# Weight slabs of half depth and double width, with a fourth place in the ring, in a two-layer decoder trunk

## The chip, the cores and the metric

The kernel runs on one core of a Trainium2 chip, in fp32 throughout. The time is the device time of one execution in microseconds (us). A core has a TensorE (PE) for matrix products, VectorE (DVE), ScalarE (ACT) and GpSimd (POOL) for the rest, and 16 DMA engines that move data between HBM and the on-chip memory SBUF. SyncE (SP) only issues transfers here. Products land in PSUM, eight banks of 512 fp32 columns by 128 partitions, written `PS[:, bank, column]`.

## The reference, cut to what matters

The trunk has 512 tokens of width 1024 and two layers. Each layer is a mixer and then a PEER channel mixer. The first mixer has gated channels and sparse attention, the second is a gated linear recurrence with 8 heads.

```python
def peer(x, w_q, sub_keys, u_tab, v_tab):
    def block(xb):
        qh = (xb @ w_q).reshape(P_TOK_BLOCK, P_HEADS, 2, P_QDIM // 2)
        s = jnp.einsum('thpd,hpnd->thpn', qh, sub_keys).astype(jnp.float32)
        s_top, i_top = lax.top_k(s, P_TOPK)
        ...
        experts = jnp.take_along_axis(cand_idx, pos, axis=-1)
        gate = jax.nn.softmax(best, axis=-1).astype(xb.dtype)
        u = u_tab[experts]
        v = v_tab[experts]
        act = jax.nn.gelu(jnp.einsum('td,thkd->thk', xb, u))
        return jnp.einsum('thk,thkd->td', gate * act, v)

def even_mixer(h, w_in, ...):
    u, v, q, kc, vc, ks, vs, kw, vw, gt = jnp.split(h @ w_in, EVEN_SPLITS, axis=-1)
    a = chunked_gmlp(jax.nn.gelu(u), jax.nn.gelu(v), a_ln_w, a_ws, a_bs)
    b = nsa(...)
    return jnp.concatenate([a, b], axis=-1) @ w_out
```

Each token thus reads 128 rows (8 heads by 16 experts) of u and v in each layer.

## The kernel before

**Slots.** The experts' work is cut into 1024 slots. A slot is one expert for each of 128 tokens: POOL gathers a row of u and v for every partition (8 KB each, 1 MB in all) into one of 8 buffers (`gath`, L646), DVE takes the dot product with x (L1282), ACT turns it into a weight and scales a diagonal matrix by it (L909, L910, L916), and PE adds the weighted v rows by two products with that diagonal (`row_product`, L1777; a few slots are added by DVE instead). A buffer comes free after that. A phase is 256 slots.

**Ticks.** All other work runs between the slots. On every engine the pieces of mixers and routings are generators that yield a tick; a piece runs ahead of the slot whose number is its tick. The 512 tokens are four blocks of 128; a mixer works on two blocks at a time ("q"), and so does a routing ("job"). The first mixer for q=0 and the routing of its first heads come before slot 0, q=1 of the first mixer has ticks 12 to 170 of phase 0, beside heads 2 to 7 of routing job 0. Routing job 1 follows late in phase 0. Phases 1 and 2 each hold one q of the second mixer and then one routing job (2 and 3), and phase 3 has slots alone.

**Slabs.** Weights come in slabs of 1 MB, loaded by SP in the fixed order of `order_` (L386), which is sorted by tick. Before slot 0 seven places in the gather buffers serve (`first_slabs`); from then on three places in `region_a`, used in turn. Before SP loads slab i it waits until the user of slab i-3 is done (`slab`), and PE waits for the landing (`slab_there`). In the first mixer the slabs of q=1 are: F 0 to 3 (keys, queries and compressed keys and values, products L1367), G (L1376), C 0 and 1 (L1390), V 0 and 1 (L1474), U 0 and 1 (L1489), O 0 to 3 (output, L1668). A routing head h needs slab R: 256 columns of `w_q` for all 8 chunks of 128 rows, and 128 KB of keys behind them (L453). F, V, U and R slabs are 256 columns wide, so each partition receives 8 pieces of 1 KB. C, O and the second mixer's H slabs are 8 KB in one piece per partition.

**Routing on PE.** Head h has four parts of four products (L1605) at ticks `route_tick(job, h)` to +3, then ACT copies the query, and at +5 four products with the keys (L1616), whose event `r_sc` frees the slab. In jobs 1 to 3 the heads are 7 ticks apart, in job 0 (from head 2) 14.

`positions_in_pairs` (L470) copies compressed keys and values within SBUF by 16 small transfers for q=1; SP issues them ahead of slab C 0.

Of the kernel before, what the change touches and what calls it, by code (L numbers as in the profile page):

```python
# [76 lines left out]
def build(nc, x, wcol_mix, w_ffn, w_fin, w_even, ln_w, ws_t, b_s, pos, ck1, ck2, cv1, cv2, w_out_e,  # L77
# [8 lines left out]
    with ExitStack() as ctx:  # L86
# [51 lines left out]
        slabs = [carve(RA, i * SLAB, SLAB) for i in range(3)]  # L138
# [100 lines left out]
        f_done, f_out, g_done, g_out = (event(n) for n in ("f_done", "f_out", "g_done", "g_out"))  # L239
# [28 lines left out]
        slab_in = [sem(f"slab_in{i}") for i in range(3)]  # L268
# [94 lines left out]
        def even_slabs(q):  # L363

            t = EVEN_AT[q]
            out_ = [(t + 12 + 8 * i, ("F", q, i), (f_done, 4 * q + i)) for i in range(4)]
            out_ += [(t + 44, ("G", q), (g_done, q))]
            out_ += [(t + 52 + 8 * kv, ("C", q, kv), ((c_half, q), (hid_done, q))[kv]) for kv in range(2)]
            out_ += [(t + 68 + 8 * i, ("V", q, i), ((v_half, q), (v_done, 2 * q + 1))[i]) for i in range(2)]
            out_ += [(t + 84 + 8 * i, ("U", q, i), ((u_half, q), (u_done, 2 * q + 1))[i]) for i in range(2)]  # L370
            return out_ + output_slabs(q, t + ATT + 48)

        def output_slabs(o, t):
            return [(t + 4 * j, ("O", o, j), (pw_used, 3 * o + j) if j < 3 else (pw_done, 4 * o + 3)) for j in range(4)]

        def routing_slabs(job):
            return [(route_tick(job, h), ("R", job, h), (r_sc, P_HEADS * job + h)) for h in range(P_HEADS)]

        def odd_slabs(q):

            out_ = [(head_tick(q, h) - 16 + half_ if h else head_tick(q, 0) - 8, ("H", q, h, half_),
                     (ig_done, C_HEADS * q + h)) for h in range(C_HEADS) for half_ in range(2)]
            return out_ + output_slabs(2 + q, head_tick(q, 7) + 3)

        first_order = even_slabs(0)
        order_ = even_slabs(1) + routing_slabs(0) + routing_slabs(1)  # L386
        for q_ in range(2):
            order_ += odd_slabs(q_) + routing_slabs(2 + q_)
        order_.sort(key=lambda e: e[0])
        first_at = {name: i for i, (_, name, _) in enumerate(first_order)}  # L390
        slab_at = {name: i for i, (_, name, _) in enumerate(order_)}
        slab_user = [user for _, _, user in order_]
        first_user = [user for _, _, user in first_order]

        def with_keys(i):
            return order_[i][1][0] == "R"

        def slab_level(i):
            return sum(16 + 16 * with_keys(j) for j in range(i % 3, i + 1, 3))

        def slab_of(*name):

            if name in first_at:
                return first_slabs[first_at[name] % 7]
            return slabs[slab_at[name] % 3]

        def slab_there(eng, *name):
# [4 lines left out]
            else:  # L412
                i = slab_at[name]
                eng.wait_ge(slab_in[i % 3], slab_level(i))
# [3 lines left out]
        def _(sp):  # L418
# [4 lines left out]
            def dram_of(name):  # L423

                kind, i = name[0], name[-1]
                if kind == "F":
                    lo = TM_ALL + (768, 0, 256, 512)[i]
                    return w_even[:, :, lo:lo + HALF]
# [4 lines left out]
                if kind == "V":  # L433
                    return w_even[:, :, 512 + i * HALF:512 + (i + 1) * HALF]
                if kind == "U":
                    return w_even[:, :, i * HALF:(i + 1) * HALF]
# [4 lines left out]
                return w_q[name[1] // 2][:, :, i * HALF:(i + 1) * HALF]  # L441

            def load(dst, name, there):
# [7 lines left out]
                if name[0] == "R":  # L451
                    _, job, h = name
# [3 lines left out]
            def first_slab(i):  # L456
# [4 lines left out]
                load(first_slabs[i % 7], first_order[i][1], first_in[i % 7])  # L461

            def slab(i):

                if i >= 3:
                    ev, n = slab_user[i - 3]
                    sp.wait_ge(ev.sem, ev.at(n))
                load(slabs[i % 3], order_[i][1], slab_in[i % 3])

            def positions_in_pairs(q):  # L470

                sp.wait_ge(f_out.sem, f_out.at(4 * q + 3))
# [32 lines left out]
            for i in range(3, len(order_)):  # L505
                if order_[i][1] == ("C", 1, 0):
                    positions_in_pairs(1)
                if order_[i][1] == ("H", 0, 0, 0):
# [146 lines left out]
        def _(act):  # L655
# [3 lines left out]
            def even_pieces(q):  # L659
# [25 lines left out]
                for i in range(4):  # L685
                    yield t0 + 20 + 8 * i
                    act.wait_ge(f_done.sem, f_done.at(4 * q + i))
                    src = v3(PS[:, 2 + i % 2, :], 2)
                    if i == 0:
                        last = a.activation(kT[:, :, q * HALF:(q + 1) * HALF], src, ACT.Copy)  # L690
                    elif i < 3:
                        last = a.activation(qT[:, 2 * i - 2:2 * i, :], src, ACT.Copy)
                    else:
                        if q == 0:
                            a.activation(kvl[:], src[:, :, HALF - CMP_STRIDE:HALF], ACT.Copy)
                        last = a.activation(kvc, src, ACT.Copy)
                    last.then_inc(f_out.sem, 1)
# [644 lines left out]
        def _(pe):  # L1342
            t = nc.tensor

            def even_pieces(q):
# [10 lines left out]
                for i in range(4):  # L1356
                    W = slab_of("F", q, i)[:, 0:KC * HALF].rearrange("p (c n) -> p c n", n=HALF)
                    for part in range(4):
                        yield t0 + 12 + 8 * i + 2 * part
                        if part == 0:  # L1360
                            slab_there(pe, "F", q, i)
                            pe.wait_ge(n_hT.sem, n_hT.at(2 * q + 1))
                            if i >= 2:
                                pe.wait_ge(f_out.sem, f_out.at(4 * q + i - 2))
                        o = part // 2
                        for c in range(4 * (part % 2), 4 * (part % 2) + 4):
                            k_ = t.matmul(PS[:, 2 + i % 2, o * HALF:(o + 1) * HALF], W[:, c, o * P:(o + 1) * P], hTe[:, c, :],  # L1367
                                          start=c == 0, stop=c == KC - 1)
                    k_.then_inc(f_done.sem, 1)
# [487 lines left out]
```

## Time and profile before

| | us |
|---|---|
| median of 3 runs | 3161.55 |
| lowest and highest | 3159.0, 3165.18 |
| the profiled execution | 3163.08 |
| its span from first to last instruction | 3161.1 |
| PE busy | 2742.0 (87%) |
| DVE, ACT, POOL busy | 2218.8, 1521.1, 1292.2 |
| gather queue q0 | 147456 packets, 1073.81 MB, 83.1% of 16 engines |
| SP's queue q1 | 69792 packets, 118.83 MB, 10.1% |

Rows of the section further down come from one profiled execution. "Idle before" in brackets is the time in which an engine waited, with what ended it. In the windows view the DMA share is the mean busy share of the 16 DMA engines. It goes a little over 1, since packets overlap, so 1.01 or 1.02 means full.

### The profile page before, as it was taken

The page shows a single profiled execution, that of the slowest core. Times are in us where ns is not written, and L with a number is a line of the kernel's source. Part 1 is how long each engine was busy: PE and PEld are TensorE (multiplying, and loading weights), DVE is VectorE, ACT ScalarE, POOL GpSimd, SP SyncE. Part 2 cuts the span into 40 slices and gives each one's busy share as a digit, 9 for nine tenths or more (in the row PEclk, how much of TensorE's full clock was granted, in tenths as well). Part 3 has the DMA queues.
Part 4 walks back from the last instruction along what each step waited for, and adds up shares of the span by engine and source line. Part 5 has one row for each costly group of instructions (what it writes and reads, how often), then busy time and mean ns, then how long its engine had stood idle before and what let it go on. Part 6 is the DMA issues. An engine that isn't in the chain of part 4 may idle for free.

```text
span 3161.1 us, 30483 instructions
## 1 busy us (share of the span) xinstructions
PE 2742.0 (87%) x8496; PEld 1484.4 (47%) x8496; DVE 2218.8 (70%) x5543; ACT 1521.1 (48%) x4080; POOL 1292.2 (41%) x1254
## 2 busy tenths in 40 slices
PE   8979789899897998889898898989999878878887
PEld 7545556344454555554465455545455422222222
DVE  1347457885766787888776788788776777676664
ACT  2334244785443556555443465565544444444443
POOL 0014234442443444445443445444544444434432
PEclk9889899999998999999999999999999999999999
DMA  8039899998999999999999999999999999999997
GB/s 290 4 116 421 316 401 390 395 345 328 403 418 422 409 378 388 382 375 398 403 421 419 421 418 363 377 402 378 396 419 417 398 427 427 427 419 421 427 427 330
DMA packets 217418, 1194.57 MB, mean 378 GB/s; under 512 B 21537, under 2 KB 77857, under 8 KB 79521
## 3 DMA queue, kind: packets, MB, share of 16 engines
q0 software_dynamic: 147456, 1073.81, 83.1%
q1 hardware_dynamic: 69792, 118.83, 10.1%
q8 instruction: 68, 1.11, 0.1%
q14 instruction: 102, 0.83, 0.1%
HBM read 1189.38 MB, written 2.10 MB: 377 GB/s over the span
## 4 chain that ended last, share of the span: by engine, by line
PE 44%; DMA 24%; DVE 14%; ACT 9%; issue 5%; POOL 3%; SPq 0%; DVEq 0%; POOLq 0%; ACTq 0%
PE ps L1777 24%; DMA region_g<-in_uv_dram,experts 18%; DVE region_g L1282 6%; DMA region_a<-in_keys_dram 6%; PE ps L1605 5%; PE ps L1637 3%; PE ps L1668 3%; POOL region_g L646 2%; ACT x_res L916 1%; PE ps L1367 1%; ACT L909 1%; PE ps L1567 1%; PE ps L1634 1%; PE ps L1685 1%; DVE region_a L1084 1%
## 5 line engine op out<-in xcount | busy, mean ns | idle before, releaser
L1777 PE MATMUL ps<-region_g,x_res 128*128 128x512 f32 x3712 | 1815.3, 621 | 270.8 <-ACT x_res L916 240.1
L646 POOL DMA_INDIRECT region_g<-in_uv_dram,experts x1024 | 1166.9, 1140 | 1651.8 <-PE ps L1777 1341.1
L1282 DVE CUSTOM_DVE_ANT_0 region_g<-region_g,region_h 128x1024 f32<-128x1024 f32 x1024 | 1256.3, 1230 | 504.3 <-DMA region_g<-in_uv_dram,experts 490.8
L1777 PEld LDWEIGHTS ps<-region_g,x_res 128*128 128x128 f32 x3712 | 689.9, 196 | 1104.1 <-issue 565.2
L909 ACT ACTIVATE region_a<-region_a 128x1 f32<-128x1 f32 x1024 | 206.5, 202 | 1249.3 <-DVE region_a L1282 1244.3
L916 ACT ACTIVATE x_res<-ident,region_a 128x128 f32<-128x128 f32 x928 | 373.3, 402 | 30.4
L910 ACT ACTIVATE region_a<-region_a,gate 128x1 f32<-128x1 f32 x1024 | 302.7, 296 | 33.4
L1605 PE MATMUL ps<-region_a 128*128 128x256 f32 x1024 | 251.7, 393 | 46.6 <-DMA region_a<-in_keys_dram 45.4
L1605 PEld LDWEIGHTS ps<-region_a 128*128 128x128 f32 x1024 | 200.2, 197 | 121.0 <-DMA region_a<-in_keys_dram 51.7
L909 ACT ACT_TABLE_LOAD x128 | 164.2, 1283 | 12.7 <-DVE region_a L1282 10.5
L1634 PE MATMUL ps<-region_a 128*128 128x256 f32 x512 | 134.0, 392 | 1.0 <-DVE region_a L1118 1.0
L1634 PEld LDWEIGHTS ps<-region_a 128*128 128x128 f32 x512 | 102.5, 201 | 66.9 <-issue 58.2
L1291 DVE SCALAR_TENSOR_TENSOR x_res<-region_g,region_a,x_res 128x1024 f32<-128x1024 f32 x96 | 123.1, 1282 | 10.4 <-ACT region_a L910 10.4
L1637 PE MATMUL ps<-region_a 128*128 128x256 f32 x512 | 129.1, 379 | 0.0
L1637 PEld LDWEIGHTS ps<-region_a 128*128 128x128 f32 x512 | 96.7, 190 | 58.0 <-issue 50.7
L1668 PE MATMUL ps<-region_a 128*128 128x512 f32 x192 | 88.8, 592 | 0.0
L1282 DVE DVE_READ_ACCUMULATOR2_ANT region_a<- 128x1 f32 x1024 | 84.7, 83 | 0.0
L901 ACT ACT_TABLE_LOAD x63 | 80.8, 1283 | 1.1
L1165 DVE SCALAR_TENSOR_TENSOR region_a<-ps,ost,region_a 128x128 f32<-128x128 f32 x32 | 9.7, 346 | 89.0 <-POOL ost L533 57.1
L1685 PEld LDWEIGHTS ps<-region_a 128*128 128x128 f32 x512 | 66.4, 191 | 10.5 <-POOL region_a L612 5.1
L1094 DVE COPY_PREDICATED region_a<-level_mask,ps 128x256 f32<-128x256 int32 x128 | 56.7, 443 | 19.9 <-PE ps L1685 11.7
L1685 PE MATMUL ps<-region_a 128*128 128x128 f32 x512 | 67.8, 276 | 2.7 <-POOL region_a L612 2.5
(233 smaller groups left out, 2305.5 us busy)
## 6 DMA issues: line engine op xcount, KB each, us to landing
region_a<-in_w_q_dram SPq DMA_DIRECT2D x32, 1024.0 KB
region_a<-in_w_odd_dram SPq DMA_DIRECT2D x32, 1024.0 KB
region_g<-in_uv_dram,experts POOLq DMA_INDIRECT x1024
region_g<-in_w_even_dram SPq DMA_DIRECT2D x8, 1024.0 KB, 8.2
region_a<-in_w_even_dram SPq DMA_DIRECT2D x8, 1024.0 KB
region_a<-in_w_out_o_dram SPq DMA_DIRECT2D x8, 1024.0 KB
region_a<-in_keys_dram SPq DMA_DIRECT2D x32, 128.0 KB
region_g<-in_w_out_e_dram SPq DMA_DIRECT2D x4, 1024.0 KB, 7.8
```

The lines of the kernel that those rows point to most:

```text
L646: g.indirect_dma_start(out=gath[:, s % NBUF, :], out_offset=None, in_=uv[s // (2 * PHASE)], in_offset=bass.IndirectOffsetOnAxis(ap=experts ...
L909: link(a.activation(gact[:, c:c + 1], dots[:, c:c + 1], ACT.Gelu_apprx_tanh))
L910: i = a.activation(wts[:, c:c + 1], gact[:, c:c + 1], ACT.Copy, scale=gate[:, n % 2, k:k + 1])
L916: a.activation(diag[:, pe_n(s) % NBUF, :], ident, ACT.Copy, scale=wts[:, c:c + 1]).then_inc(diag_ready.sem, 1)
L1282: v.tensor_tensor_reduce(out=u_, in0=u_, in1=XNr[n // P_HEADS % 3], scale=1.0, scalar=0.0, op0=ALU.mult, op1=ALU.add, accum_out=dots[:, c: ...
L1291: v.scalar_tensor_tensor(xb, gath[:, s % NBUF, D_MODEL:ROW], wts[:, c:c + 1], xb, ALU.mult, ALU.add).then_inc(vd_done.sem, 1)
L1605: i = t.matmul(PS[:, 4, p * HALF:(p + 1) * HALF], W[:, c, p * P:(p + 1) * P], hTh[:, c, :], start=c == 0, stop=c == KC - 1)
L1634: i = t.matmul(PS[:, 2, o * HALF:(o + 1) * HALF], W[:, c % 4, o * P:(o + 1) * P], hTh[:, c, :], start=c == 0, stop=c == KC - 1)
L1637: i = t.matmul(PS[:, 3, o * HALF:(o + 1) * HALF], hTh[:, c, o * P:(o + 1) * P], W[:, c % 4, HALF:2 * HALF], start=c == 0, stop=c == KC - 1)
L1668: i = t.matmul(PS[:, out_bank(o, bank), :], headT[:, c, r * P:(r + 1) * P], W[:, c % 2, half_ * 512:(half_ + 1) * 512], start=c == 0, stop ...
L1685: i = t.matmul(PS[:, 4 + pair % 2, (lev % 2) * HALF + r * P:(lev % 2) * HALF + (r + 1) * P], k_, q_, start=True, stop=True)
L1777: i = t.matmul(PS[:, j, :], diag[:, pe_n(s) % NBUF, :], gath[:, s % NBUF, D_MODEL + j * 512:D_MODEL + (j + 1) * 512], start=first, stop=last)
```

## The change

R, V and U slabs and two of the F slabs now hold 4 chunks of 128 rows instead of 8, and 512 columns instead of 256, so a partition receives 4 pieces of 2 KB. The bytes of a slab stay the same. Two routing heads share a pair of such slabs (`("R", job, pair, half)`): both heads need both, the keys of the even head lie behind the first and those of the odd head behind the second. The first half is freed by the odd head's `r_q`, the second by its `r_sc`. In jobs 1 to 3 odd heads run one tick earlier. F 2 and F 3 hold all queries and add up into banks 6, 7, 2 and 3; F 1 now holds the compressed keys and values, so `positions_in_pairs` waits for `f_out` 1 instead of 3 and is issued ahead of F 3. V and U products are 512 columns wide, half as many. A fourth place lies over `headT`, used in the first mixer of q=1 alone from `pw_done` 3 on (all output pieces of q=0 done). The order of phase 0 and the place of each slab are written by hand; later ones use three places in turn.

```diff
-        slabs = [carve(RA, i * SLAB, SLAB) for i in range(3)]
+        slabs = [carve(RA, i * SLAB, SLAB) for i in range(3)] + [carve(RA, 3 * SLAB + KC * HALF, KC * HALF)]
...
-            return NORM_TICK[job] + 9 + 7 * h
+            return NORM_TICK[job] + 9 + 7 * h - h % 2
...
+        def routing_slabs(job, pair):
+            n = P_HEADS * job + 2 * pair + 1
+            return [(("R", job, pair, 0), (r_q, n)), (("R", job, pair, 1), (r_sc, n))]
...
+        order_ = [(*R0[0][0], 0), (*R0[0][1], 1), (*F0, 2), (*F1, 3), (*R0[1][0], 0), (*R0[1][1], 1), (*F2, 2),
+                  (*R0[2][0], 0), (*R0[2][1], 1), (*F3, 3), (*G_, 2), (*C0, 3), (*R0[3][0], 0), (*R0[3][1], 1), (*C1, 2),
+                  (*V0, 3), (*V1, 2), (*U0, 3), (*U1, 2), (*O0, 0), (*O1, 1), (*O2, 2), (*O3, 0)]
...
+        order_ += [(*e, (i + 1) % 3) for i, e in enumerate(later)]
...
-                sp.wait_ge(f_out.sem, f_out.at(4 * q + 3))
+                sp.wait_ge(f_out.sem, f_out.at(4 * q + 1))
...
-                if order_[i][1] == ("C", 1, 0):
+                if order_[i][0] == ("F", 1, 3):
                     positions_in_pairs(1)
...
+                for half_ in range(2):
+                    W = slab_of("F", q, 2 + half_)[:, 0:KC * HALF].rearrange("p (c n) -> p c n", n=2 * HALF)
+                    for part in range(4):
+                        yield t0 + 28 + 8 * half_ + 2 * part
+                        if part == 0:
+                            slab_there(pe, "F", q, 2 + half_)
+                        if part >= 2:
+                            pe.wait_ge(f_out.sem, f_out.at(4 * q + part - 2))
+                        for c in range(4 * half_, 4 * half_ + 4):
+                            k_ = t.matmul(PS[:, (6, 7, 2, 3)[part], 0:HALF], W[:, c % 4, part * P:(part + 1) * P], hTe[:, c, :],
+                                          start=c == 0, stop=c == KC - 1)
...
+                        pe.wait_ge(f_out.sem, f_out.at(4 * q + 2))
...
                         yield route_tick(job, h) + part
+                        if part < 2:
+                            slab_there(pe, "R", job, h // 2, part)
```

On SP, from the last slab of q=0 on, the order before was this (`in_w_even` with 8x256 is F, with 8x280 G; `in_w_q` is R):

```order
L450 DMA region_a<-in_w_even_dram 128x8x256 [waits r_sc]
L450 DMA region_a<-in_w_q_dram 128x8x256 [waits r_sc]
L453 DMA region_a<-in_keys_dram 128x256
L450 DMA region_a<-in_w_even_dram 128x8x256 [waits r_sc]
L450 DMA region_a<-in_w_even_dram 128x8x256 [waits f_done]
L450 DMA region_a<-in_w_q_dram 128x8x256 [waits r_sc]
L453 DMA region_a<-in_keys_dram 128x256
L450 DMA region_a<-in_w_even_dram 128x8x256 [waits f_done]
L450 DMA region_a<-in_w_even_dram 128x8x280 [waits f_done]
```

These are F 0, R of head 3, F 1, F 2, R of head 4, F 3 and G. Now, from the same place on (F 0 is loaded before):

```order
L459 DMA region_a<-in_w_even_dram 128x8x256 [waits pw_done]
L459 DMA region_a<-in_w_q_dram 128x4x512 [waits r_q]
L463 DMA region_a<-in_keys_dram 128x256
L459 DMA region_a<-in_w_q_dram 128x4x512 [waits r_sc]
L463 DMA region_a<-in_keys_dram 128x256
L459 DMA region_a<-in_w_even_dram 128x4x512 [waits f_done]
L459 DMA region_a<-in_w_q_dram 128x4x512 [waits r_q]
L463 DMA region_a<-in_keys_dram 128x256
L459 DMA region_a<-in_w_q_dram 128x4x512 [waits r_sc]
L463 DMA region_a<-in_keys_dram 128x256
L488 DMA region_a<-region_h 64x256 [waits f_out]
```

These are F 1, the pair of heads 2 and 3, F 2, the pair of heads 4 and 5, and the first of the 16 small transfers, which now stand ahead of F 3.

On PE, head 4 of job 0 began like this, with one wait for its slab (`slab_in1`) ahead of its first part:

```order
L1367 MATMUL ps<-region_a 128x256 x4
L1605 MATMUL ps<-region_a 128x256 [waits r_qo,r_hT,slab_in1]
L1605 MATMUL ps<-region_a 128x256 x3
L1777 MATMUL ps<-region_g,x_res 128x512 [waits diag_ready]
L1777 MATMUL ps<-region_g,x_res 128x512
L1605 MATMUL ps<-region_a 128x256 x4
```

Now:

```order
L1389 MATMUL ps<-region_a 128x256 x4
L1632 MATMUL ps<-region_a 128x256 [waits r_qo,r_hT,slab_in0]
L1632 MATMUL ps<-region_a 128x256 x3
L1804 MATMUL ps<-region_g,x_res 128x512 [waits diag_ready]
L1804 MATMUL ps<-region_g,x_res 128x512
L1632 MATMUL ps<-region_a 128x256 [waits slab_in1]
```

The head's first part waits for the first half of its pair, and the second part, one row product later, for the second half.

## Rows read from the trace of the kernel before

**Rows 1.** Page, DMA queues: packets, MB, share of 16 engines' span

```profile
q0 software_dynamic: 147456, 1073.81, 83.1%
q1 hardware_dynamic: 69792, 118.83, 10.1%
```

**Rows 2.** Windows: busy of each engine, granted clock, DMA share, GB/s

```profile
core 0: us, PE busy (x) PEld busy (x) DVE busy (x) ACT busy (x) POOL busy (x), PEclk, DMA share, GB/s
...
300.00:400.00 100.00, 76.12 (x258) 50.16 (x257) 52.46 (x135) 27.87 (x82) 26.11 (x25) 0.88 0.89 332
400.00:500.00 100.00, 89.68 (x356) 57.39 (x356) 60.09 (x150) 41.80 (x117) 33.34 (x32) 0.95 0.98 383
...
620.00:780.00 160.00, 149.02 (x450) 69.34 (x449) 118.87 (x275) 116.30 (x274) 68.98 (x73) 0.97 0.88 331
...
1540.00:1740.00 200.00, 182.63 (x583) 107.21 (x583) 139.67 (x337) 86.29 (x246) 87.76 (x74) 0.97 1.02 419
...
2500.00:3100.00 600.00, 477.51 (x958) 171.97 (x956) 423.37 (x1071) 262.54 (x784) 252.33 (x247) 0.97 1.01 425
```

**Rows 3.** Windows of 20 us within phase 0, same columns

```profile
300.00:320.00 20.00, 10.40 (x37) 6.55 (x35) 14.74 (x43) 6.50 (x21) 6.18 (x6) 0.89 1.02 418
320.00:340.00 20.00, 14.48 (x47) 10.22 (x48) 7.57 (x20) 2.58 (x6) 1.92 (x3) 0.77 0.64 224
340.00:360.00 20.00, 20.00 (x73) 13.01 (x72) 7.36 (x11) 9.32 (x27) 9.07 (x8) 1.00 0.92 343
...
380.00:400.00 20.00, 20.00 (x71) 13.79 (x71) 9.73 (x26) 3.86 (x10) 4.62 (x5) 0.90 0.83 269
...
480.00:500.00 20.00, 20.00 (x77) 13.77 (x76) 17.45 (x48) 10.80 (x27) 7.37 (x7) 1.00 0.87 310
```

**Rows 4.** Waits from 234 to 500 us: total, times, longest

```profile
POOL region_g L646 <- PE ps L1777: 164.0, 60, 19.5
...
PE ps L1605 <- DMA region_a<-in_keys_dram: 32.6, 3, 15.1
```

**Rows 5.** Timeline of PE in phase 0: start, length, line, idle before

```profile
308.51 1.89 PE L1367 MATMUL ps<-region_a 128*128 128x256 f32 x8
325.52 3.78 PE L1605 MATMUL ps<-region_a 128*128 128x256 f32 x8 [15.13 <-DMA region_a<-in_keys_dram]
...
330.91 1.89 PE L1605 MATMUL ps<-region_a 128*128 128x256 f32 x8
...
349.02 1.89 PE L1367 MATMUL ps<-region_a 128*128 128x256 f32 x8
...
378.74 3.78 PE L1605 MATMUL ps<-region_a 128*128 128x256 f32 x8 [8.76 <-DMA region_a<-in_keys_dram]
...
391.88 1.89 PE L1605 MATMUL ps<-region_a 128*128 128x256 f32 x8
...
422.45 1.89 PE L1605 MATMUL ps<-region_a 128*128 128x256 f32 x8
```

**Rows 6.** Timeline of PE, last two heads of routing job 2

```profile
1702.91 1.99 PE L1605 MATMUL ps<-region_a 128*128 128x256 f32 x8 [2.14 <-DMA region_a<-in_keys_dram]
...
1726.42 3.78 PE L1605 MATMUL ps<-region_a 128*128 128x256 f32 x8 [5.14 <-DMA region_a<-in_keys_dram]
```

**Rows 7.** Windows: routing slabs beside gathers, and gathers alone

```profile
1678.00:1697.00 19.00, 17.65 (x64) 11.02 (x63) 12.20 (x26) 8.95 (x23) 8.07 (x7) 1.00 1.02 417
2600.00:2800.00 200.00, 161.61 (x324) 57.34 (x322) 139.81 (x360) 87.75 (x263) 80.61 (x80) 0.97 1.01 427
```

**Rows 8.** Timeline of SP: slab issues in phase 0 and in routing job 2

```profile
250.15 28.95 SPq L450 DMA_DIRECT2D region_a<-in_w_even_dram  x2
...
1621.51 0.55 SPq L450 DMA_DIRECT2D region_a<-in_w_q_dram  x1
...
1639.61 0.55 SPq L450 DMA_DIRECT2D region_a<-in_w_q_dram  x1
```

**Rows 9.** Page, DMA issues: an 8 KB load, us from issue to landing

```profile
lbraw<-in_lbs_dram SPq DMA_DIRECT2D x1, 8.0 KB, 4.4
```

More of the change, by code:

```diff
@@ L363, in even_slabs @@
         def even_slabs(q):
[L365 to L377, printed above, removed]
+            out_ = [(("F", q, i), ((f_done, 4 * q), (f_done, 4 * q + 1), (f_half, q), (f_done, 4 * q + 3))[i]) for i in range(4)]
+            out_ += [(("G", q), (g_done, q))]
@@ L387, in build @@
-        for q_ in range(2):
[L388 to L399, printed above, removed]
+        F0, F1, F2, F3, G_, C0, C1, V0, V1, U0, U1, O0, O1, O2, O3 = even_slabs(1)
@@ new lines, in build @@
+        R0 = [routing_slabs(0, pair) for pair in range(4)]
+        order_ = [(*R0[0][0], 0), (*R0[0][1], 1), (*F0, 2), (*F1, 3), (*R0[1][0], 0), (*R0[1][1], 1), (*F2, 2),
+                  (*R0[2][0], 0), (*R0[2][1], 1), (*F3, 3), (*G_, 2), (*C0, 3), (*R0[3][0], 0), (*R0[3][1], 1), (*C1, 2),
+                  (*V0, 3), (*V1, 2), (*U0, 3), (*U1, 2), (*O0, 0), (*O1, 1), (*O2, 2), (*O3, 0)]
+        later = [e for pair in range(4) for e in routing_slabs(1, pair)]
+        for q_ in range(2):
+            later += odd_slabs(q_) + output_slabs(2 + q_)
+            later += [e for pair in range(4) for e in routing_slabs(2 + q_, pair)]
@@ new lines, in build @@
+        order_ += [(*e, (i + 1) % 3) for i, e in enumerate(later)]
+        order_ = [(name, slot, user) for name, user, slot in order_]
+        first_at = {name: i for i, (name, _) in enumerate(first_order)}
+        slab_at = {name: i for i, (name, _, _) in enumerate(order_)}
+        first_user = [user for _, user in first_order]
+        slab_before, slab_level, users, levels = [], [], [None, None, None, (pw_done, 3)], [0] * 4
+        for name_, slot_, user_ in order_:
+            slab_before.append(users[slot_])
+            users[slot_] = user_
+            levels[slot_] += 16 + 16 * (name_[0] == "R")
+            slab_level.append(levels[slot_])
@@ L440, in dram_of @@
                     return w_odd[name[2]][:, i * 2048:(i + 1) * 2048]
-                return w_q[name[1] // 2][:, :, i * HALF:(i + 1) * HALF]
+                _, job, pair, half_ = name
+                return w_q[job // 2][:, 4 * half_:4 * half_ + 4, pair * 512:(pair + 1) * 512]
             def load(dst, name, there):
@@ L451, in load @@
                 if name[0] == "R":
-                    _, job, h = name
+                    _, job, pair, half_ = name
+                    h = 2 * pair + half_
                     sp.dma_start(dst[:, KC * HALF:SLAB].rearrange("p (a b) -> p a b", a=2),
@@ L696, in even_pieces @@
                         last = a.activation(kvc, src, ACT.Copy)
+                    else:
+                        bank = (6, 2)[i - 2]
+                        last = a.activation(qT[:, 2 * i - 4:2 * i - 2, :], PS[:, bank:bank + 2, 0:HALF], ACT.Copy)
                     last.then_inc(f_out.sem, 1)
```

83 lines of the change are left out of this document (44 added, 39 removed).

## The prediction, written before the result was known

> **What bounds the kernel now.** I first read the DMA queues and the DMA share by stretch, then who stops whom where that share falls. Two queues share the 16 DMA engines: the gathers take 83.1% of the engines' time and SP's loads 10.1% [rows 1]. In the last phase, with gathers alone, the share is full and 425 to 427 GB/s flow [rows 2, 7]. During routing job 2 (1540 to 1740 us) it is full too, at 419 GB/s [rows 2]. So there DMA sets the time, and only fewer or cheaper bytes help. In phase 0 it isn't full: 0.89 from 300 to 400 us and 0.98 to 500 [rows 2]. Full is 1.02 here, and the four low windows of 20 us hold 20 x (0.38 + 0.10 + 0.19 + 0.15) = 16.4 us of idle DMA [rows 3]. From 620 to 780 us, at 0.88, PE is 93% busy with attention [rows 2], which this change doesn't touch.
>
> What leaves DMA idle in phase 0 is PE. From 234 to 500 us PE waits almost only three times, 32.6 us in all, for a routing slab whose keys come last, and POOL stands up to 19.5 us with no buffer free [rows 4]. Two of these waits are 15.13 and 8.76 us, and the four products after each take 3.78 us instead of 1.89 [rows 5]: the granted clock was at its lower level (1.2 GHz of 2.4) after the idle time, at 0.77 of full over 320 to 340 us [rows 3]. With 1.9 us for each, the waits cost PE 32.6 + 5.7 = 38.3 us.
>
> **Why the slabs come late.** In job 2 the last two heads both start on a landing, at 1702.91 and 1726.42 us [rows 6]: one slab of 1152 packets of 1 KB (keys included) per 23.5 us. At 417 GB/s [rows 7] 9.8 MB flow in that time, 1.18 MB of them slab, so the gathers move 8.6 MB, or 1055 packets of 8 KB. The engines thus alternate, about 1.09 slab packets for one gather packet. A gather packet takes 8192 B / (427/16 GB/s) = 307 ns. The 16 engines have 376 us in 23.5 us, so a 1 KB packet takes (376 - 1055 x 0.307) / 1152 = 45 ns.
>
> **Part 1, packets of 2 KB.** No row has one alone. It costs between 77 ns (bytes at the gathers' rate) and 90 ns (twice 45). I take 82, on the line through 45 and 307. A slab then needs 512 x 82 / 16 = 2.62 us of all engines instead of 2.88, or 0.26 us less (0 to 0.4). Beside gathers it lands in (512/1.09 x 0.307 + 512 x 0.082) / 16 = 11.6 us, plus 2.6 for the keys (an eighth of the old 20.9), so 14.2 instead of 23.5. The Trainium skill (Perfetto Trace Analysis, DMA Optimizations) says that transfers under 2 KB have a large overhead each and that batching them raises throughput a lot. By the line above the overhead of a packet is some 7 ns, and 0.26 us a slab is all the throughput there is; more of it would only add to the gain.
>
> **Part 2, jobs 1 to 3.** DMA is full, so 24 slabs give 24 x 0.26 = 6.3 us (0 to 9). A new wait comes with the pairs: the second half of the next pair is requested when the odd head's projection ends (`r_q`) and is needed 6 ticks later by the second part of the next head. A tick is 18.1/7 = 2.59 us (issues at 1621.51 and 1639.61 us [rows 8]), so there are 15.5 us. The load needs 4.4 us of latency (small load, [rows 9]) + 14.2 = 18.6. PE waits some 3 us, and up to 1.9 more where the clock falls. The loop from one `r_q` to the next is then 18.6 + 8 ticks (20.7) + 1.9 = 41.2 us at most, while DMA needs 14 gathers x 2.46 + 2 slabs x 2.98 = 40.4 for the same slots. The two are level and buffered by 8 gathers, so I book 0 for it (0 to 2 us for each of 9 waits). Behind the waiting PE stand row products, and behind those POOL's free buffers; SP's H slabs are asked for 4 ticks later and used 24 ticks on.
>
> **Part 3, phase 0.** F 1 and the pair of heads 2 and 3 are requested before or about the first gather, and the second half (14.2 + 4.4 us) is there by the time of head 2's second part. Then step by step, on the clock of before. F 2 is issued at 278.6 us as now (end of the double row at 250.15, [rows 8]), lands at 279 + 3 + 11.6 = 294, the first half of heads 4 and 5 at 308, the second at 322.5, and with the end of its latency PE has it at 325. PE reaches it after the F part at 308.51, one head part and one row product [rows 5], at 313.7: a wait of 11.5 us. At 325 it then starts the second part, which before ran at 330.91 [rows 5], so it is 5.5 us ahead. Next in the queue stand 16 small transfers, 1024 packets of at most 1 KB. Beside gathers they would hold F 3 back by 20.9 us, alone by 3. PE has just stood still for 11 us, which 8 buffers hardly outlast, so the gather queue is nearly dry: I take 3. F 3 lands by 341; PE needs it 349.02 - 330.91 = 18.1 us after 325 [rows 5], at 343: a wait of 0 to 14, I take 2. G is still 1 KB wide, issued two ticks earlier than the use of F 3, and just makes it: 0 to 4, I take 2. Head 5 shares head 4's pair, so the wait at 378.74 is gone, and so is the one at head 7. For heads 6 and 7 both halves are asked for within 5 us, the first at head 5's `r_q` (393.8, the end of the part at 391.88), and both are in after 4.4 + 2 x 14.2 = 32.8 us; PE is at the place of 422.45 after 28.7 [rows 5]: 4 us. Sum of waits: 11.5 + 2 + 2 + 4 = 19.5, and 3.8 for the clock at two of them, 23.3 in place of 38.3. PE gains 15 us. DMA: 16.4 idle + 11 slabs x 0.26 = 19.3 at most, less some 5 that stay idle after the 11.5 us wait and the later ones, 14. Neither limit lets more through than the smaller, and they won't mesh fully: I take 12 (bounds 0 and 19).
>
> **Part 4, the rest.** Before slot 0 nothing waits on a slab; the F, V and U products keep their columns (256 wide, eight rows in 1.73 us; 512 wide, twice that), and G's new wait for ACT's copy is covered by eight F products. Fewer weight loads run beside products. 0, bounds +-2. The fourth place waits for `pw_done` 3, which comes before head 0's keys; ACT writes `headT` again only after U 0. After 500 us the order of slabs is the old one.
>
> **Sum.** 12 + 6 = 18 us from the profiled execution's 3163.1, so 3145; the median lies 1.5 lower, so 3143.5, which I round to 3143.
>
> **The rivals.**
> (a) New waits eat phase 0. If the small transfers do meet live gathers, F 3 comes 14 us late, G behind it 4 or more, and PE's sum is 23.3 + 14 = 37 against 38.3. Only the 6 us of part 2 stay, or fewer: 3155 to 3162. For it: the second half lands when gathers restart. Against: POOL's 19.5 us without a buffer [rows 4].
> (b) DMA fills nearly everywhere: the full 19 in phase 0, 9 in the jobs, and a few from the drained spell after job 3: 3130 to 3135.
> (c) Slower: the share goes by bytes, not by packets, or the rows are split into 1 KB again. A slab then still needs 23.5 us, and the pairs turn this into a loss: the loop is 27.9 + 20.7 + 1.9 = 50.5 us against 40.4, over three waits in three jobs 91 us, of which 8 buffered slots a job (20 us) hide up to 60: about +30, so 3190. It decides from a landing time of about 13.5 us on, where the loop passes DMA's 40.4; my 14.2 is close to that, so even the expected time has a small loss in it. Against it: 1152 to 1055 packets is one to one in number and 1 to 7.3 in bytes, which a share by bytes would hit only by chance. The Trainium skill (DMA: Bandwidth & Descriptors, Queues, rings and completion order) says that an engine changes rings only after a whole packet of typically 9 to 17 descriptors; where such packets are cut by bytes, this rival follows, at its 3190. The profile's one to one count speaks for turns by the single row, or equal numbers of rows.
>
> **How the numbers follow.** Forecast 0.58 (3138 to 3155), (a) 0.22, (b) 0.10, (c) and other losses 0.10. Low 3128 takes in (b), high 3163 takes in (a), which leaves out about 0.17. A measurement of this kernel tells some 0.2%, 6 us, from no change. Faster by more: forecast, (b) and a quarter of (a), 0.73. Within: 0.16. Slower: 0.11.
>
> **What would show it.** Right: 2 KB packets at 80 to 85 ns; in jobs 1 to 3 short PE waits (3 to 5 us) at the second part of heads 2, 4 and 6, with the DMA share still at 1.02; in phase 0 one wait of about 11 us at head 4's second part, none at heads 5 and 7, and 500 us of before reached near 488. Wrong: long waits at F 3 or G (a), landings still 23 us apart (c), or a share under 1 inside the jobs, which would mean that the pair loop and not DMA sets the pace there.

## The result and the profile after

The change made the kernel slower, where a gain of 0.6% was forecast.

| | median, us | lowest to highest | runs |
|---|---|---|---|
| before | 3161.55 | 3157.35 to 3166.11 | 7 |
| after | 3184.69 | 3175.39 to 3196.53 | 7 |

The ratio is 1.0066, with a 95% interval of 1.0046 to 1.0086, so the loss is small but clear of no change. The profiled execution of after took 3188.32 us, its span is 3186.4. The forecast was 3143 with a range of 3128 to 3163, so the time lies outside of the range and on the other side of no change.

First the queues, from the page of after (packets, MB, share of 16 engines). They answer to [rows 1]:

```profile
q0 software_dynamic: 147456, 1073.81, 83.2%
q1 hardware_dynamic: 47264, 118.83, 9.8%
```

The change does what it says: the same bytes in fewer packets on SP's queue, which now takes 9.8% of a longer span instead of 10.1%.

Next the costliest line of routing, from the page's groups of instructions (busy us, mean ns of one, then idle time before them and what ended it). Before, the same group read 251.7, 393 and 46.6, of which 45.4 for the keys' DMA:

```profile
L1632 PE MATMUL ps<-region_a 128*128 128x256 f32 x1024 | 262.7, 405 | 79.0 <-DMA region_a<-in_keys_dram 77.8
```

PE waits 77.8 us for routing slabs, 32 us more than before, although the routing slabs have fewer packets. Where these waits are is told by the view of waits on PE, a window at a time: phase 0 (234 to 500 us), then the three later jobs:

```profile
PE ps L1632 <- DMA region_a<-in_keys_dram: 12.2, 2, 11.1
...
PE ps L1632 <- DMA region_a<-in_keys_dram: 23.6, 3, 8.2
...
PE ps L1632 <- DMA region_a<-in_keys_dram: 22.7, 3, 8.5
...
PE ps L1632 <- DMA region_a<-in_keys_dram: 19.3, 3, 8.3
```

Phase 0 has 12.2 us where it had 32.6 [rows 4]. The jobs have 19 to 24 us each, in three waits each. Before, the same view shows none in job 1, 7.3 us in job 2 (the last two heads, [rows 6]) and 5.5 us in job 3.

The timeline of PE for job 1 (start, us, line, operation, [idle before <- releaser]) has the three waits, at the second part of heads 2, 4 and 6:

```profile
857.66 3.78 PE L1632 MATMUL ps<-region_a 128*128 128x256 f32 x8 [8.20 <-DMA region_a<-in_keys_dram]
...
904.94 3.78 PE L1632 MATMUL ps<-region_a 128*128 128x256 f32 x8 [7.17 <-DMA region_a<-in_keys_dram]
...
951.81 3.78 PE L1632 MATMUL ps<-region_a 128*128 128x256 f32 x8 [8.21 <-DMA region_a<-in_keys_dram]
```

The distances are 47.3 and 46.9 us. In job 2 the same three stand at 1628.35, 1674.88 and 1722.72, in job 3 at 2394.41, 2440.64 and 2483.97. A pair of heads thus takes 43 to 48 us, most often 47, where DMA needs 40.4 by the forecast's own sum.

Does DMA still set the pace there? The view by windows says no. Its columns are the window, its length, the busy time of the five engines, the clock, the DMA share and GB/s. Of before:

```profile
820.00:990.00 170.00, 158.40 (x534) 96.12 (x534) 112.51 (x279) 70.23 (x203) 73.47 (x63) 0.98 1.01 415
1520.00:1760.00 240.00, 219.36 (x682) 124.23 (x680) 162.36 (x393) 98.95 (x290) 106.53 (x92) 0.97 1.02 418
2280.00:2500.00 220.00, 203.26 (x641) 117.04 (x640) 149.54 (x351) 92.30 (x265) 95.45 (x85) 0.97 1.01 409
```

And of after, with phase 0 ahead:

```profile
300.00:400.00 100.00, 88.88 (x315) 57.66 (x314) 58.57 (x144) 37.88 (x107) 35.68 (x32) 0.95 0.99 388
400.00:500.00 100.00, 97.68 (x338) 54.05 (x337) 73.44 (x179) 41.68 (x119) 41.82 (x39) 1.00 1.02 423
...
820.00:990.00 170.00, 146.42 (x488) 91.53 (x487) 100.32 (x237) 61.83 (x184) 64.14 (x55) 0.93 0.96 370
1520.00:1760.00 240.00, 209.91 (x655) 122.34 (x654) 151.20 (x362) 91.50 (x268) 93.17 (x85) 0.94 0.97 388
2280.00:2500.00 220.00, 192.93 (x598) 111.35 (x597) 144.62 (x353) 85.36 (x256) 88.12 (x78) 0.95 0.98 391
```

Phase 0 went from 332 and 383 GB/s [rows 2] to 388 and 423. The jobs went the other way, from 409 to 418 down to 370 to 391. The share of 0.97 instead of 1.02 looks harmless; the rate shows a loss of 4 to 11%. These windows are the same in time and not in work. Taken from slot to slot (192 to 272, 464 to 544, 704 to 800), the rates are 411, 420 and 414 GB/s before and 381, 386 and 394 after, a loss of 5 to 8%.

To see what each stage gave or took, I compare the time at which POOL issues the gather of the same slot (its 1024 gathers are one instruction each, L646 before, L657 after). Here are slot 272 of before and then of after, in the timeline of POOL:

```profile
1044.00 1.31 POOL L646 DMA_INDIRECT region_g<-in_uv_dram,experts  x1 [0.30 <-issue]
...
1038.49 1.00 POOL L657 DMA_INDIRECT region_g<-in_uv_dram,experts  x1 [0.31 <-issue]
```

All differences are after minus before, in us, and the columns to the right are for three of the experiments below:

| slot | lies | before, at | after | narrow_late | four_places | late_pairs_alone |
|---|---|---|---|---|---|---|
| 96 | late in phase 0's slabs | 522.5 | -25.8 | -22.4 | -26.3 | -0.6 |
| 192 | ahead of job 1 | 819.0 | -21.3 | -19.7 | -21.4 | -0.8 |
| 272 | behind job 1 | 1044.0 | -5.5 | -22.7 | -29.9 | +11.7 |
| 464 | ahead of job 2 | 1612.8 | -4.7 | -24.1 | -27.5 | +16.3 |
| 704 | ahead of job 3 | 2315.2 | +12.3 | -23.9 | -31.2 | +29.9 |
| 800 | behind job 3 | 2574.8 | +25.4 | -26.4 | -36.7 | +43.3 |

So phase 0 gave 21 to 26 us. Each stretch with a job in it took 13 to 17 (15.8, 17.0, 13.1), which is 46 in all, and the end is 25 later.

### The profile page after: what moved, and what is told of

The parts are those of the page before. It is cut to its first block, busy times and chain, and to the rows that moved or that the text cites. A ratio compares the mean times of both kernels' runs of the same rounds, so it can differ in the third digit from the quotient of the medians.

```text
span 3186.4 us, 30231 instructions
## 1 busy us (share of the span) xinstructions
PE 2744.5 (86%) x8368; PEld 1463.9 (46%) x8368; DVE 2218.2 (70%) x5543; ACT 1515.2 (48%) x4080; POOL 1293.4 (41%) x1254
## 4 chain that ended last, share of the span: by engine, by line
PE 47%; DMA 24%; DVE 13%; ACT 9%; issue 4%; POOL 3%; SPq 0%; POOLq 0%; DVEq 0%; ACTq 0%
PE ps L1804 24%; DMA region_g<-in_uv_dram,experts 16%; PE ps L1632 7%; DMA region_a<-in_keys_dram 6%; DVE region_g L1294 6%; PE ps L1664 3%; PE ps L1695 2%; POOL region_g L657 1%; ACT L921 1%; ACT x_res L928 1%; PE ps L1661 1%; PE ps L1591 1%; PE ps L1712 1%; PE ps L1500 1%; ACT region_a L922 1%
## 5 line engine op out<-in xcount | busy, mean ns | idle before, releaser
L657 POOL DMA_INDIRECT region_g<-in_uv_dram,experts x1024 | 1166.2, 1139 | 1675.9 <-PE ps L1804 1422.2
L1632 PE MATMUL ps<-region_a 128*128 128x256 f32 x1024 | 262.7, 405 | 79.0 <-DMA region_a<-in_keys_dram 77.8
L1632 PEld LDWEIGHTS ps<-region_a 128*128 128x128 f32 x1024 | 206.9, 204 | 157.5 <-DMA region_a<-in_keys_dram 86.5
L1661 PE MATMUL ps<-region_a 128*128 128x256 f32 x512 | 135.3, 395 | 1.0 <-DVE region_a L1130 1.0
L1661 PEld LDWEIGHTS ps<-region_a 128*128 128x128 f32 x512 | 102.7, 201 | 67.0 <-issue 58.1
L1664 PE MATMUL ps<-region_a 128*128 128x256 f32 x512 | 129.1, 379 | 0.0
L1664 PEld LDWEIGHTS ps<-region_a 128*128 128x128 f32 x512 | 96.7, 190 | 58.0 <-issue 50.7
L835 ACT ACTIVATE region_a<-ps 128x512 f32<-128x512 f32 x32 | 19.1, 597 | 190.9 <-PE ps L1632 190.9
L1712 PEld LDWEIGHTS ps<-region_a 128*128 128x128 f32 x512 | 66.4, 191 | 12.4 <-POOL region_a L623 6.9
```

What stands on the lines that cost most here:

```text
L657: g.indirect_dma_start(out=gath[:, s % NBUF, :], out_offset=None, in_=uv[s // (2 * PHASE)], in_offset=bass.IndirectOffsetOnAxis(ap=experts ...
L1632: i = t.matmul(PS[:, 4, p * HALF:(p + 1) * HALF], W[c // 4][:, c % 4, h % 2 * HALF + p * P:h % 2 * HALF + (p + 1) * P], hTh[:, c, :], star ...
L1661: i = t.matmul(PS[:, 2, o * HALF:(o + 1) * HALF], W[:, c % 4, o * P:(o + 1) * P], hTh[:, c, :], start=c == 0, stop=c == KC - 1)
L1664: i = t.matmul(PS[:, 3, o * HALF:(o + 1) * HALF], hTh[:, c, o * P:(o + 1) * P], W[:, c % 4, HALF:2 * HALF], start=c == 0, stop=c == KC - 1)
L1712: i = t.matmul(PS[:, 4 + pair % 2, (lev % 2) * HALF + r * P:(lev % 2) * HALF + (r + 1) * P], k_, q_, start=True, stop=True)
```

## What could explain it, and the experiments

**The loop (L).** The second half slab of the next pair is requested when the odd head's projection ends, lands a while later, is needed by the next even head's second part, and only then can PE work on to the next such request. This loop takes longer than DMA needs for the same slots, so it sets the pace. It goes away when the second half has a place of its own ahead of time, or when the jobs have no pairs.

Against it stood that the wide slabs or their packets cost the time wherever they run (C), and that the loss comes from what the change moved in phase 0 (D). In phase 0 itself the question was whether the 2 KB packets (P) or the hand-written order with its shared pairs and fourth place (O) brought the gain. Every kernel below was timed beside before, whose medians were 3163.16 (first four) and 3163.81 us (last three).

### narrow_late: the jobs as they were, phase 0 as changed

```diff
-            return NORM_TICK[job] + 9 + 7 * h - h % 2
+            return NORM_TICK[job] + 9 + 7 * h
...
-        later = [e for pair in range(4) for e in routing_slabs(1, pair)]
+        later = [(("N", 1, h), (r_sc, P_HEADS + h)) for h in range(P_HEADS)]
...
+                if kind == "N":
+                    return w_q[name[1] // 2][:, :, i * HALF:(i + 1) * HALF]
```

> The changed kernel with routing jobs 1 to 3 as before (one slab of all 8 chunks and 256 columns for each head, heads 7 ticks apart); phase 0 stays as changed. Theory L (loop): in jobs 1 to 3 the second half of a pair is asked for only at the odd head's projection, and landing plus PE's work up to the next such point (46.7 us a pair) passes what DMA needs (40.4); this costs 20, 19 and 13 us in the three jobs. It expects the whole of it back and the 24 us of phase 0 kept: 3136 to 3141 us. Theory C (contention): the 2 KB packets of any slab slow gathers and PE wherever they run, and phase 0 gained in spite of it. It expects the same here. Rival D (downstream): the lead won in phase 0 is given back later whatever the jobs do: about 3161.

Measured: 3138.34 us (3135.28 to 3142.82), ratio 0.992 with 0.989 to 0.9951. The loss of after is gone, and what is left is the gain of phase 0. The difference to after is 46 us in the medians and 52 us between the two traces at slot 800; most of it is the 46 of the jobs in the table, and narrow_late gains another 7 us on before from slot 192 to slot 800. So nothing that phase 0 does at its new places costs time later, and D is out. The three jobs have PE waits of 1.39 and 5.09, of 3.21, and of 1.16 and 4.32 us, 15 us in all, near the 13 of before. So the pairs of jobs 1 to 3 are the cause; how they cost it is for the next five.

### late_pairs_alone: the other way round

The kernel before, with pairs and the odd heads' early tick in jobs 1 to 3 alone.

```diff
-            return NORM_TICK[job] + 9 + 7 * h
+            return NORM_TICK[job] + 9 + 7 * h - h % 2
...
+            return [(route_tick(job, 2 * p_) + half_ / 4, ("R", job, p_, half_),
+                     ((r_q, r_sc)[half_], P_HEADS * job + 2 * p_ + 1)) for p_ in range(4) for half_ in range(2)]
```

> The kernel before with one part of the change: pairs of half slabs in 2 KB packets and odd heads one tick early in routing jobs 1 to 3, three places. Phase 0 is as before. Theory L (loop) expects the same waits of about 8 us at the second parts of heads 2, 4 and 6, and the sum of what the three jobs lost, 20 + 19 + 13 = 50 us on top of before: 3205 to 3215 us. A theory by which the jobs lost only because phase 0 had run ahead (and met a different queue) expects 3161 to 3175.

Measured: 3205.08 us (3201.65 to 3209.8), ratio 1.0115 with 1.006 to 1.017, 41 us more than before: the lower edge of what L expected. The timeline of PE shows three waits in job 2 at the same places, where L had some 8 us for each:

```profile
1649.67 3.55 PE L1621 MATMUL ps<-region_a 128*128 128x256 f32 x8 [8.45 <-DMA region_a<-in_keys_dram]
...
1695.56 6.22 PE L1621 MATMUL ps<-region_a 128*128 128x256 f32 x16 [6.15 <-DMA region_a<-in_keys_dram]
...
1739.87 3.78 PE L1621 MATMUL ps<-region_a 128*128 128x256 f32 x8 [5.35 <-DMA region_a<-in_keys_dram]
```

Over the three jobs the nine waits are 5.3 to 8.5 us. The two parts of the change add up but for 7 us: +41 here and -25 in narrow_late give +16, against +23 for both. What makes these 7 us is not shown; the 95% interval of this run's ratio alone is 17 us to either side.

### four_places: pairs of 2 KB, but the second half asked for a pair ahead

The place over `headT` is used in jobs 1 to 3 too, for the second half of every odd pair (the keys of its odd head go to 256 free columns at the end of `region_a`). The three others take turns among the rest. All packets are as in after; the places differ, and with them the moment of the request.

```diff
+        keys3 = carve(RA, 18784 - HALF, HALF)
...
-        order_ += [(*e, (i + 1) % 3) for i, e in enumerate(later)]
+        turn = 1
+        for e in later:
+            if e[0][0] == "R" and e[0][2] % 2 and e[0][3]:
+                order_.append((*e, 3))
+            else:
+                order_.append((*e, turn % 3))
+                turn += 1
```

> The changed kernel, pairs of half slabs with 2 KB packets in all jobs, but the second half of every odd pair lies in the fourth place (with the odd head's keys behind the mixers' data), so that a whole pair can be loaded while the one before is in use. Theory L expects the three waits of about 8 us per job at the second part of heads 2, 4 and 6 gone or under 2 us, a full DMA share in the jobs, and 3136 less up to 6 for cheaper packets: 3130 to 3137 us. Theory C expects the loss to stay, since the packets are the same: about 3185.

Measured: 3126.47 us (3124.01 to 3131.81), ratio 0.9883 with 0.9852 to 0.9914. That is 58 us faster than after with the same packets, and 4 us better than the range that L gave. In the waits of PE from 820 to 1030 us there is none for a slab any more; the longest group left is this:

```profile
PE ps L1814 <- ACT x_res L937: 9.7, 9, 2.9
```

and the windows of the jobs are full:

```profile
820.00:990.00 170.00, 155.12 (x513) 91.42 (x511) 114.94 (x276) 70.88 (x209) 72.51 (x63) 0.99 1.01 423
1520.00:1760.00 240.00, 212.64 (x661) 118.33 (x659) 170.12 (x399) 106.97 (x302) 104.98 (x95) 0.97 1.02 424
```

423 and 424 GB/s, against 415 and 418 before and 418 and 419 in narrow_late. From slot 192 to 272 it is 423 against 411 and 413, so it isn't the choice of window: here the 2 KB packets at last bring what the forecast promised for DMA. Against narrow_late the gain is 12 us, 6.3 of which are the packets by the forecast's Part 2 (an estimate; no run has it alone); the rest may be the 15 us of waits that narrow_late's jobs still have and this one's don't.

### four_no_shift: the same without the early tick

```diff
-            return NORM_TICK[job] + 9 + 7 * h - h % 2
+            return NORM_TICK[job] + 9 + 7 * h
```

> The kernel of four_places with heads 7 ticks apart as before, so without the odd heads' one tick. With the pairs loaded well ahead the tick has nothing left to do. Expected: the same as four_places, 3124 to 3130 us; more than 4 us either way would mean that PE's order in the jobs matters by itself.

Measured: 3125.39 us (3121.54 to 3126.83), ratio 0.9865 with 0.9813 to 0.9917. Level with four_places, so the tick does nothing once the slab is there in time. These two are the fastest versions, better than both kernels.

### pairs_1kb: the loop, with a longer landing

Each half slab of jobs 1 to 3 comes as two transfers of 256 columns, so its packets are 1 KB again.

```diff
-                sp.dma_start(d_, src).then_inc(there, 16)
+                if name[0] == "R" and name[1] > 0:
+                    sp.dma_start(d_[:, :, 0:HALF], src[:, :, 0:HALF]).then_inc(there, 16)
+                    sp.dma_start(d_[:, :, HALF:2 * HALF], src[:, :, HALF:2 * HALF]).then_inc(there, 16)
```

> The changed kernel, but in jobs 1 to 3 each half slab is loaded by two transfers of 256 columns, so in 1 KB packets; pairs, places and releases stay. Theory L expects the half slab to land after 28 us instead of 19, a pair to take 56 us instead of 46.7, waits of about 17 us, and 9 x 9.2 us more: 3245 to 3268 us. Theory C expects the loss to go with the 2 KB packets: 3140 to 3165.

Measured: 3240.66 us (3237.59 to 3248.79), ratio 1.0238 with 1.0208 to 1.0268. The waits of job 1:

```profile
867.43 3.78 PE L1637 MATMUL ps<-region_a 128*128 128x256 f32 x8 [13.94 <-DMA region_a<-in_keys_dram]
...
920.15 3.68 PE L1637 MATMUL ps<-region_a 128*128 128x256 f32 x8 [12.10 <-DMA region_a<-in_keys_dram]
...
972.11 3.78 PE L1637 MATMUL ps<-region_a 128*128 128x256 f32 x8 [13.82 <-DMA region_a<-in_keys_dram]
```

The period grew from 47 to 52.3 us, and the waits from 8 to 13.3. From its request at 842.32 us to its use at 867.43 the slab takes 25.1 us, against 19.4 in after: the longer landing goes into the loop one for one. Theory C expected the loss to go, and it grew by 56 us. A theory in which the place or the width of the slab costs the time has no reason for this. L had the landing at 28 us, the waits at 17 and the period at 56, all too long, so the time came out below its 3245 to 3268.

### odd_early3: the same loop, cut differently

Odd heads run three ticks earlier instead of one.

```diff
-            return NORM_TICK[job] + 9 + 7 * h - h % 2
+            return NORM_TICK[job] + 9 + 7 * h - 3 * (h % 2)
```

> The changed kernel with the odd heads of jobs 1 to 3 three ticks early instead of one; nothing else. The odd head's projection ends two ticks sooner after its even head's. Theory L expects each pair to be shorter by two row products (3.4 us), 9 times: about 3154 to 3162 us, with waits at the even heads' second part longer (10 to 12 us), since two slots' work moves behind the request's landing only in part. Theory C expects no change: 3180 to 3190.

Measured: 3150.03 us (3138.57 to 3152.19; two of the six executions took 3139), ratio 0.9942 with 0.9919 to 0.9965. That is 4 us below the expected range. Two waits in job 1:

```profile
856.19 2.74 PE L1632 MATMUL ps<-region_a 128*128 128x256 f32 x8 [4.05 <-DMA region_a<-in_keys_dram]
...
940.64 3.78 PE L1632 MATMUL ps<-region_a 128*128 128x256 f32 x8 [3.80 <-DMA region_a<-in_keys_dram]
```

The text expected longer waits, 10 to 12 us, and they became shorter: a miss, and one of sign. Worked out from the rows it is plain. The odd head's projection, and with it the request, comes two ticks earlier (at 837.53 in SP's timeline of this kernel), so PE has 14.6 us of work until it needs the slab instead of 11.2, and the wait shrinks by 3 to 4 us; the work from the second part to the next request shrinks by as much. The landing is as before (18.7 us), and two turns take 84.5 us, or 42.2 each, near DMA's 40.4. Both waits are 4 us, head 4's is gone, and from slot 192 to slot 800 the lead on before falls only from 18.7 to 11.4 us: the jobs take 7 us in all instead of 46. One number of the schedule, 3 in place of 1, thus gives back 35 us with the same slabs, places and packets. That speaks for the loop and against every theory about the slabs themselves.

### phase0_1kb: phase 0 without the 2 KB packets

narrow_late with the wide slabs of phase 0 loaded as two transfers of 256 columns each. Order, pairs and fourth place stay.

```diff
-                sp.dma_start(d_, src).then_inc(there, 16)
+                if (name[0] == "R" or name[0] in "VU" and name[1] == 1 or name[0] == "F" and name[1] == 1 and name[2] >= 2):
+                    sp.dma_start(d_[:, :, 0:HALF], src[:, :, 0:HALF]).then_inc(there, 16)
+                    sp.dma_start(d_[:, :, HALF:2 * HALF], src[:, :, HALF:2 * HALF]).then_inc(there, 16)
```

> The kernel of narrow_late (phase 0 as changed, jobs 1 to 3 as before), but the wide slabs of phase 0 (routing pairs, F 2, F 3, V, U of q=1) are loaded by two transfers of 256 columns each, so in 1 KB packets; order, places and releases stay. Theory P (packets): the 24 us won in phase 0 come from slabs that land in 12 us instead of 21 beside gathers. It expects most of them lost: the second half of heads 4 and 5 lands about 27 us later, and PE waits some 35 us there and again at heads 6 and 7: 3160 to 3190 us. Theory O (order): they come from two heads sharing a pair, the fourth place and the early loads, whatever the packets. It expects 3138 to 3145 us.

Measured: 3152.1 us (3143.74 to 3155.99), ratio 0.9958 with 0.9935 to 0.9981. It lies between the two theories. PE's waits in phase 0:

```profile
327.06 3.78 PE L1645 MATMUL ps<-region_a 128*128 128x256 f32 x8 [13.01 <-DMA region_a<-in_keys_dram]
...
424.99 3.78 PE L1645 MATMUL ps<-region_a 128*128 128x256 f32 x8 [12.18 <-DMA region_a<-in_keys_dram]
...
522.43 3.63 PE L1521 MATMUL ps<-region_a 128*128 128x512 f32 x4 [2.09 <-DMA region_a<-in_w_even_dram]
```

In narrow_late the first two were 9.80 and 3.43. Slot 96 is 8.3 us ahead of before here and 22.4 there, so 14 us of phase 0's gain come from the 2 KB packets and 8 from the rest. Of the 14, up to 3 would be their cheaper bytes (11 slabs at the forecast's 0.26 us, an estimate), the others the earlier landing; the run doesn't part the two. How the 8 are shared by the order, the pairs and the fourth place was not tried and stays open.

## Why the prediction was wrong, point by point

**The failing step: "needed 6 ticks later", "A tick is 18.1/7 = 2.59 us", "so there are 15.5 us" (Part 2).** The place, the mechanism and the landing time in this step were right; the price of the ticks was not. SP's timeline in after has the two requests (the half slab, then its keys) that open two turns of the loop:

```profile
838.29 0.38 SPq L459 DMA_DIRECT2D region_a<-in_w_q_dram  x1
838.71 0.51 SPq L463 DMA_DIRECT2D region_a<-in_keys_dram  x1
...
884.89 0.38 SPq L459 DMA_DIRECT2D region_a<-in_w_q_dram  x1
```

and PE's timeline has what lies behind the first, up to the wait at 857.66 shown above:

```profile
836.37 1.89 PE L1632 MATMUL ps<-region_a 128*128 128x256 f32 x8
838.10 3.60 PE L1804 MATMUL ps<-region_g,x_res 128*128 128x512 f32 x8
841.53 1.05 PE L1643 MATMUL ps<-region_a 128*128 128x128 f32 x8
842.42 5.32 PE L1804 MATMUL ps<-region_g,x_res 128*128 128x512 f32 x12
847.57 1.89 PE L1632 MATMUL ps<-region_a 128*128 128x256 f32 x8
```

The odd head's projection ends at 838.26. Six ticks later PE is done with everything up to head 2's second part at 849.46: 11.2 us, made of five row products (1.72 each), one product with keys (0.9) and one part of a head (1.7 to 1.9). The slab is used at 857.66, 19.4 us after its request, where 18.6 was forecast (eight of the nine turns have 18.9 to 20.1 us, the last of job 3 has 15.7). So the wait is 8.2 instead of "some 3". From 857.66 to the next request at 884.89 PE has 27.2 us, where the forecast had 20.7 + 1.9 = 22.6. The whole turn is 19.4 + 27.2 = 46.6 us, not 41.2, against 40.4 of DMA.

| | forecast | measured |
|---|---|---|
| request to use (landing) | 18.6 | 19.4 |
| PE's work in that time | 15.5 | 11.2 |
| wait | 3 | 8.2 |
| use to next request | 22.6 | 27.2 |
| a turn of the loop | 41.2 | 46.6 |

The mean of 2.59 us mixes dear and cheap ticks. Four of seven carry a part of a head (3.44 us with the row product), one carries the keys (2.6), two carry a row product alone (1.7); about one slot in seven goes to DVE and has none, which brings the mean to 2.59. The stretch behind `r_q` holds the cheap ones, and the one ahead of it the dear ones, of which an odd head's four stand in a row. The profile of before had all this. PE's timeline in job 2 there, from the end of one head to the end of the next:

```profile
1615.26 1.89 PE L1605 MATMUL ps<-region_a 128*128 128x256 f32 x8
1620.42 1.05 PE L1616 MATMUL ps<-region_a 128*128 128x128 f32 x8
1623.03 1.89 PE L1605 MATMUL ps<-region_a 128*128 128x256 f32 x8
1626.48 1.89 PE L1605 MATMUL ps<-region_a 128*128 128x256 f32 x8
...
1633.36 1.89 PE L1605 MATMUL ps<-region_a 128*128 128x256 f32 x8
```

From 1617.15 (the end of `r_q`'s part) to 1626.48 are 9.3 us, and the odd head's early tick adds a row product of 1.7: 11.0. From 1626.48 to the end of the part at 1633.36 are 8.8, plus a head of 18.1, less 1.7: 25.2. The loop is 18.6 + 25.2 + 1.9 = 45.7, so 5.3 us too long in each of nine turns, or 48 us. Measured are 46 (after against narrow_late) and 41 (late_pairs_alone against before). Put in at Part 2, this gives 3143 + 48 = 3191. With the true gain of phase 0 (24 for 12), and without the 6 us that DMA can't give where it is starved, the sum is 3185.

**"buffered by 8 gathers, so I book 0 for it"** fell with it. Little was hidden: 18.6 us of excess per job by the measured turn (three times 46.6 less 40.4; in job 3 one turn is only 43.3), against 15.8, 17.0 and 13.1 us lost. Eight buffers can hide a late landing once, but here not a loop that is longer than the bound in every turn.

**Rival (c)** named the loop, and the point "from about 13.5 us on" from which it decides. It was given 0.10 since I tied it to a landing of 23.5 us. The landing is 15.0 us (19.4 less 4.4), and the loop lost all the same. The sentence "my 14.2 is close to that, so even the expected time has a small loss in it" should have moved the chances.

The turns between the queues did go by the row, as the forecast had it. With a share by bytes the slab should not have landed 6 us earlier with 2 KB packets (19.4 us) than with 1 KB ones (25.1 in pairs_1kb). The packet records of before show the turns themselves. They name no engine, but each packet starts 3 to 5 ns ahead of the end of another, which strings them into 16 chains. From 1682 to 1696 us, 1299 of the 1377 steps in these chains go from one queue to the other: one gather packet, then one slab packet. The Trainium skill (DMA: Bandwidth & Descriptors, Queues, rings and completion order) has an engine drain 9 to 17 descriptors from one ring before it changes; this trace doesn't agree with that, if a packet of the profile is one descriptor.

**Part 1 was right.** The landing is 19.4 against 18.6, and by the packet records of after a 2 KB packet takes 84 ns (median; the mean is 89) and one of 1 KB 46 ns (50), against 82 and 45.

**Part 2's gain of 6.3 us** for DMA fits the runs once the loop is gone: four_places is 12 us ahead of narrow_late, as said above, though no run has it alone. In after it can't show, since DMA no longer sets the pace in the jobs.

**Part 3 was right in its steps and too small in its sum.** The wait at head 4's second part was forecast at 325 us with 11.5 us. The timeline of PE in after has all three waits for slabs in phase 0:

```profile
325.45 3.78 PE L1632 MATMUL ps<-region_a 128*128 128x256 f32 x8 [11.12 <-DMA region_a<-in_keys_dram]
...
408.62 1.99 PE L1632 MATMUL ps<-region_a 128*128 128x256 f32 x8 [1.10 <-DMA region_a<-in_keys_dram]
413.55 1.09 PE L1416 MATMUL ps<-region_a 128*128 128x32 f32 x8 [1.22 <-DMA region_a<-in_cv_dram]
```

No wait at heads 5 and 7, as forecast, and none at F 3 and G, where 2 us each were booked; heads 6 and 7 have 1.1 instead of 4. The last wait, for slab C 1, was not in the forecast. Waits and the slow four products come to 13.4 + 1.9 = 15.3 us instead of 23.3, so PE gains 23 and not 15. That is what came: 21 to 26 us, twice the 12 that I took; what ran at 500 us before runs at 474 and not at 488. The other limit, "DMA: 16.4 idle + 11 slabs x 0.26 = 19.3 at most", was wrong too. It was read from the busy share, and the share hides a part of the loss. Over the slabs of phase 0, before (217 to 522.5 us) and after (217 to 496.7, the same slots), the windows read:

```profile
217.00:522.50 305.50, 260.17 (x930) 165.93 (x931) 187.20 (x454) 115.72 (x324) 108.69 (x102) 0.92 0.96 379
...
217.00:496.70 279.70, 254.01 (x886) 154.64 (x887) 187.53 (x452) 115.50 (x324) 114.48 (x102) 0.95 1.01 410
```

By the share, 0.96 against a full 1.02, 18 us could be won of 305.5. By the rate, 379 against the 419 of a full stretch [rows 2], it is 305.5 x (1 - 379/419) = 29 us. 26 came, so the rate was nearer.

**Part 4 and rivals (a) and (b).** Nothing in the runs speaks against the 0 of Part 4; it wasn't measured alone. Rival (a) did not happen: the gather queue was nearly dry, as assumed (11 packets from 328 to 332 us, beside 955 of SP's queue), and F 3 was there in time. Rival (b), DMA full nearly everywhere at 3130 to 3135, did not come with this change; four_places comes nearest to it, at 3126, with a full share in phase 0 and the jobs, but still 0.91 from 620 to 780 us.

## What to carry to other kernels

- Where a request, its landing, the work behind it and the next request form a loop, add up its turn and compare it with what the bound needs for the same work. A turn that is too long costs its excess every time; here 8 buffers hid 2 to 3 us of 19 per job. Price each leg by the instructions that stand in it, not by a mean per tick: here the same 14 ticks split into 11 and 25 us where the mean said 15.5 and 20.7.
- Halves that are both needed at once want both places ahead of time. One more place for 1 MB, free in that stretch anyway, turned a loss of 0.7% into a gain of 1.2 to 1.35%.
- Read the room that a starved DMA leaves from GB/s against a full stretch, not from its busy share.

## What the runs showed of the hardware that was not expected

A DMA engine's busy share isn't proportional to what it moves when its queue runs thin. The share of before over 217 to 522.5 us is 0.96 at 379 GB/s, or 395 GB/s for a full share; in four_places' job 1 it is 1.01 at 423, or 419. In after's job 1, where PE's waits starve the gathers, it is 0.96 at 370, or 385. The packets themselves become longer there: by all packet records of that first stretch, a gather packet of 8 KB takes 322 ns on average in before and 314 in after, against 310 in the last phase. In after's job 1 (820 to 990 us) it takes 337, where four_places has 310 in the same window. The median is 309 ns in every one of these, so it is a part of the packets that takes much longer. What makes them longer was not tried.
